# Moving fifteen pairs of gathered rows from the spreading units into the units of pass B's blocks

## The chip, the cores and the metric

The kernel runs on one core of one Trainium2 chip. The metric is the device time of one execution in microseconds. A core has TensorE (PE, the matmuls, with its weight loads as PEld), VectorE (DVE), ScalarE (ACT), GpSimd (POOL), SyncE (SP) and 16 DMA engines that all queues share.

## The reference, cut to what matters

One layer of a trunk over 1024 positions and 1024 features. The second half of it is a product-key expert layer (PEER): each position has 8 heads, and each head picks 16 of 16384 experts.

```python
s1, i1 = lax.top_k(s[:, :, 0], PEER_TOPK); s2, i2 = lax.top_k(s[:, :, 1], PEER_TOPK)
top_s, sel = lax.top_k(cand_s, PEER_TOPK)
idx = jnp.take_along_axis(cand_i, sel, axis=-1)
gate = jax.nn.softmax(top_s, axis=-1)
u = jnp.take(expert_u, idx, axis=0)
act = jax.nn.gelu(jnp.einsum('thkd,td->thk', u, xb))
v = jnp.take(expert_v, idx, axis=0)
return jnp.einsum('thk,thkd->td', gate * act, v)
```

Before it come a gMLP block, a short convolution and an output projection, each with a share of one large input projection.

## The kernel before, in words

The 1024 positions are two groups: A has 3 blocks of 128 positions, B has 5. The expert layer is computed in two ways. For B it is dense: every expert's `u` row is multiplied with every position (64 units of kind E), the chosen gates are **spread** into a dense matrix by one-hot matmuls, and the product is multiplied with every expert's `v` row (64 units of kind W). For A it is sparse: 384 **slots** (3 blocks x 8 heads x 16 experts), and each slot needs one gathered row of `expert_u` and one of `expert_v` for each of 128 positions, 128 rows of 4 KB a gather. So there are 768 gathers, issued by POOL as indirect DMAs (L743), each into a buffer of a ring. DVE uses up each one with one instruction of 128x1024 fp32: a dot product for a `u` row (L1136) or a weighted sum into `acc_sp` for a `v` row (L1145). The buffer is free again after that instruction.

TensorE works through a fixed list of units, `UNITS`. A front unit or an E unit has 96 matmuls of 320 columns (four PSUM tiles; every operand is split into a high and a low fp16 part, which makes three products). In the order of time, for B: V, C, U (4 units), M (16 units, the merged gated products), O (5 blocks, one after another), Q, E, W. The gathers of A are laid beside B's units: `_sections()` gives each unit a number k of slots, and the section of a unit is then about k `u` rows and k `v` rows. The `u` rows run 32 slots ahead of the `v` rows (`LAG`).

The order on each engine is written out by hand, and each engine works strictly in order:

- **DVE, in an M unit**: at odd units the merge (L1290 at u%4 = 1; L1292, L1294, L1297, L1299 at u%4 = 3), which waits for the evacuation of the unit's PSUM tiles; then all rows of the unit's section. After M15's rows come the five blocks of O (`o_block_B`: residual, two layer norms), and then the high and low parts that Q is multiplied with (L1111). The first O block needs x for B, loaded at L660 once M15's tiles are done.
- **ACT, in an M unit**: it evacuates the PSUM tiles into three buffers, which DVE's merges set free.
- **ring of buffers**: 8 buffers for rows in units U and M (`front`), 4 in Q0 and Q1, 6 in the spreading units (`spread`).
- **SP, in U and M**: a 1 MB load of a unit's weights from `hl_dram` (L595), issued four units ahead, when the tiles of the unit that used the buffer before are done.
- **spreading units**: E40 to E59 (`E_SPREAD` = 40, `N_SPREAD` = 20). Beside its 96 matmuls each has 8 spreads of 8 small matmuls (L1922) into `psX`, four PSUM tiles in rotation; ACT copies each spread to `gbuf` (L750, Z<-psX). DVE makes the one-hots, per spread one L1493 and one L1500, and between these it takes rows of the section, one at every second spread. At the end of a unit ACT issues the 2 MB store of `gbuf` (L983, `g_dram`, pieces of 512 bytes) and right behind it the store of the unit's activations (L987, `a_dram`), both on ACT's own DMA queue. Only then does it go on to the copies of the next unit. SP loads 1 MB of `u` weights a unit (L586), which ACT and DVE split (L750, L1040).

Of the kernel before, what the change touches and what calls it, by code (L numbers as in the profile page):

```python
# [191 lines left out]
E_SPREAD = 2 * NGRP - N_SPREAD - 4  # L192
# [12 lines left out]
def _sections():  # L205

    k = {("B", "U", u): 0 for u in (1, 2, 3)}
    for u in range(16):
        k["B", "M", u] = (3 + u % 2) * (u > 0)
    for h in range(HEADS):  # L210
        k["B", "Q", h] = 2 + (h > 1)
    for e in range(2 * NGRP):
        k["B", "E", e] = 2 + e % 2 if e < E_SPREAD - 4 else 2
    groups = NGRP - 2
    left = SLOTS - sum(k.values())
    for g in range(groups):
        k["B", "W", 2 * g] = left * (g + 1) // groups - left * g // groups
    return k

SECTION = _sections()
SEC_UNITS = [u for u in UNITS if u in SECTION]
SEC_OF = {u: c for c, u in enumerate(SEC_UNITS)}
# [1801 lines left out]
```

## Time and profile before

| | us |
|---|---|
| median of 3 runs (lowest, highest) | 2948.1 (2935.65, 2956.32) |
| the profiled execution: its own time | 2951.08 |
| its span, first to last instruction | 2949.3 |
| PE busy | 2828.4 (96%) |
| DVE busy | 2514.4 (85%) |
| ACT busy | 879.7 (30%) |
| POOL busy | 1009.1 (34%) |
| all DMA, mean over the span | 311 GB/s |

### The profile page before, as it was taken

How to read it: one execution, taken by the hardware profiler on the slowest of the kernel's cores; microseconds unless marked ns; L12 is line 12 of the kernel's file. 1: busy time of each engine (PE TensorE's matmuls, PEld its weight loads, DVE VectorE, ACT ScalarE, POOL GpSimd, SP SyncE). 2: the span in 40 equal slices, each digit the busy share in tenths (PEclk: the TensorE clock that was granted, in tenths of full speed). 3: DMA queues.
4: the chain of work that ended last, by engine and by line, in shares of the span. 5: the costliest groups of instructions: out<-in, count | busy, mean ns of one | idle time of the engine just before them, and what ended most of it. 6: DMA issues, size and time to landing. Idle time of an engine off the chain costs nothing.

```text
span 2949.3 us, 47374 instructions
## 1 busy us (share of the span) xinstructions
PE 2828.4 (96%) x19184; PEld 1840.3 (62%) x19184; DVE 2514.4 (85%) x4708; ACT 879.7 (30%) x1321; POOL 1009.1 (34%) x778
## 2 busy tenths in 40 slices
PE   4999999998999899999999989999999999999998
PEld 4566686776677777777776667776544444444443
DVE  6876566987887889999999999997699999999877
ACT  3333542221111342222222334443222222222223
POOL 0000000002776025444445522222465556555410
PEclk9999999999999999999999999999999999999999
DMA  8989653433999468888888899999999999999973
GB/s 328 346 327 379 239 188 129 143 123 131 396 386 379 171 234 313 308 307 316 325 324 321 331 313 327 335 343 309 366 415 414 411 397 411 395 409 403 354 264 136
DMA packets 266236, 917.54 MB, mean 311 GB/s; under 512 B 20465, under 2 KB 102433, under 8 KB 222753
## 3 DMA queue, kind: packets, MB, share of 16 engines
q1 hardware_dynamic: 63968, 427.91, 37.3%
q0 software_dynamic: 110592, 402.70, 36.4%
q10 hardware_dynamic: 91456, 83.89, 8.4%
q8 instruction: 152, 2.49, 0.3%
q14 instruction: 68, 0.55, 0.1%
HBM read 771.79 MB, written 142.63 MB: 310 GB/s over the span
## 4 chain that ended last, share of the span: by engine, by line
PE 37%; DVE 9%; DMA 4%; ACTq 3%; issue 2%; POOL 1%; ACT 1%; DVEq 0%; POOLq 0%
PE psU L1715 6%; PE psU L1716 6%; PE psU L1717 6%; PE psX L1715 5%; PE psX L1717 5%; PE psX L1716 5%; ACTq L987 3%; DMA rows<-in_v_rows,idx_sp 3%; PE psX L1922 2%; DVE acc_sp L1145 2%; DVE w L1040 1%; DMA Z<-in_v_rows,idx_sp 1%; POOL rows L743 1%; DVE rows L1136 1%; DVE Z L1371 1%
## 5 line engine op out<-in xcount | busy, mean ns | idle before, releaser
L1715 PE MATMUL psU<-hB,w 128*128 128x320 f16 (+2 forms) x3104 | 929.8, 300 | 25.3 <-ACT Z L750 11.7
L1716 PE MATMUL psU<-hB,w 128*128 128x320 f16 (+2 forms) x3104 | 929.7, 300 | 0.0
L1717 PE MATMUL psU<-hB,w 128*128 128x320 f16 (+2 forms) x3104 | 929.3, 300 | 0.0
L750 ACT ACTIVATE w<-stage 128x2048 f16<-128x2048 f32 x176 | 335.8, 1909 | 658.9 <-PE psX L1717 347.1
L1040 DVE SCALAR_TENSOR_TENSOR w<-stage,w 128x2048 f16<-128x2048 f32 x176 | 402.6, 2289 | 113.4 <-ACT w L750 113.2
L743 POOL DMA_INDIRECT rows<-in_u_rows,idx_sp x200 | 271.1, 1356 | 382.2 <-DVE rows L1136 234.7
L1715 PEld LDWEIGHTS psU<-hB,w 128*128 128x128 f16 x3104 | 305.8, 99 | 138.9 <-issue 20.8
L1717 PEld LDWEIGHTS psU<-hB,w 128*128 128x128 f16 x3104 | 305.9, 99 | 118.7
L1716 PEld LDWEIGHTS psU<-hB,w 128*128 128x128 f16 x3104 | 305.8, 99 | 111.0
L743 POOL DMA_INDIRECT rows<-in_v_rows,idx_sp x205 | 254.7, 1242 | 277.9 <-DVE rows L1136 178.5
L1715 PE MATMUL psX<-w,Z 128*128 128x512 f16 x768 | 291.1, 379 | 2.5 <-DVE Z L1636 1.4
L1716 PE MATMUL psX<-w,Z 128*128 128x512 f16 x768 | 291.1, 379 | 0.0
L1717 PE MATMUL psX<-w,Z 128*128 128x512 f16 x768 | 291.1, 379 | 0.0
L1145 DVE SCALAR_TENSOR_TENSOR acc_sp<-rows,weight_sp,acc_sp 128x1024 f32<-128x1024 f32 x205 | 258.0, 1288 | 31.9 <-DMA rows<-in_v_rows,idx_sp 26.1
L1715 PE MATMUL psU<-w,Z 128*128 128x512 f16 (+1 forms) x768 | 264.6, 344 | 5.1 <-ACT acc_sp L750 2.6
L1716 PE MATMUL psU<-w,Z 128*128 128x512 f16 (+1 forms) x768 | 264.4, 344 | 0.0
L1717 PE MATMUL psU<-w,Z 128*128 128x512 f16 (+1 forms) x768 | 264.4, 344 | 0.0
L1136 DVE SCALAR_TENSOR_TENSOR rows<-rows,h_sp 128x1024 f32<-128x1024 f32 x200 | 239.2, 1219 | 11.5 <-DMA rows<-in_u_rows,idx_sp 10.3
L750 ACT ACTIVATE R<-psU 128x320 f32<-128x320 f32 (+1 forms) x296 | 123.4, 430 | 310.0 <-PE psU L1717 309.9
L1715 PE MATMUL psU<-Z,w 128*128 128x384 f16 (+1 forms) x640 | 205.7, 321 | 5.7 <-DVE w L1040 5.7
L750 ACT ACTIVATE Z<-psU 128x320 f32<-128x320 f32 (+3 forms) x228 | 96.5, 446 | 367.6 <-PE psU L1717 337.1
L1716 PE MATMUL psU<-Z,w 128*128 128x384 f16 (+1 forms) x640 | 205.6, 321 | 0.0
(262 smaller groups left out, 4432.2 us busy)
## 6 DMA issues: line engine op xcount, KB each, us to landing
stage<-in_u_units SPq DMA_DIRECT2D x64, 1024.0 KB, 8.7
stage<-in_v_units SPq DMA_DIRECT2D x64, 1024.0 KB, 8.0
stage<-in_w_front SPq DMA_DIRECT2D x48, 1024.0 KB, 9.1
hl_dram<-w SPq DMA_DIRECT2D x48, 1024.0 KB, 7.0
w<-hl_dram SPq DMA_DIRECT2D x48, 1024.0 KB, 7.3
a_dram<-R ACTq DMA_DIRECT2D x64, 640.0 KB, 8.0
g_dram<-Z ACTq DMA_DIRECT2D x20, 2048.0 KB, 16.0
Z<-a_dram SPq DMA_DIRECT2D x32, 1280.0 KB, 11.8
```

What stands on the lines that cost most here:

```text
L743: pool.indirect_dma_start(row_at[r], None, u_rows if table == "u" else v_rows, bass.IndirectOffsetOnAxis(ap=idx_sp[:, slot:slot + 1], axis ...
L750: return nc.scalar.activation(dst, src, func, scale=scale)
L987: act.dma_start(a_dram[u // 2, :, 2 * (u % 2):2 * (u % 2) + 2, :], v3(a_ring[:, u % 4, :], 2)).then_inc(a_stored[u % 4], 16)
L1040: V.scalar_tensor_tensor(w[:, n % NW, 1, :], stage[:, v % 2, :], WS, w[:, n % NW, 0, :], ALU.mult, ALU.subtract).then_inc(lo_done, 1)
L1136: V.scalar_tensor_tensor(row_at[r], row_at[r], 1.0, h2_sp[:, slot % SB, :], ALU.mult, ALU.mult, accum_out=dots[:, c % 8, j:j + 1]).then_in ...
L1145: V.scalar_tensor_tensor(dst, row_at[r], weight_sp[:, slot:slot + 1], dst, ALU.mult, ALU.add).then_inc(row_used, 1)
L1371: step(V.max_index(p[:, 8:16], v[:, 8:16], s))
L1715: mm(ps, lhs[0](k), rhs[0](k), start=start and s == 0, stop=False)
L1716: mm(ps, lhs[0](k), rhs[1](k), start=False, stop=False)
L1717: last = mm(ps, lhs[1](k), rhs[0](k), start=False, stop=stop and s == n - 1)
L1922: ins = mm(ps[:, t * P:(t + 1) * P], oh_keys[:, q % 4, t // 2, 0, :, t % 2], oh_gate[:, q % 4, t // 2, c, :, t % 2], start=(c == 0), stop= ...
```

## The change

The number of slots beside an M unit goes from 3 or 4 to 4 or 5 (15 units, M1 to M15), and the number beside E40 to E54 from 2 to 1. E55 to E59 and all other units keep theirs: the W units get what is left of 384 slots, and that is the same number. With the lag, M1 to M15 together get 15 `u` rows and 15 `v` rows more, and E40 to E54 15 of each fewer. Section by section: an odd M unit goes from 4 + 4 rows to 5 + 5, an even one from 3 + 3 to 4 + 4, a spreading unit up to E54 from 2 + 2 to 1 + 1.

```diff
     for u in range(16):
-        k["B", "M", u] = (3 + u % 2) * (u > 0)
+        k["B", "M", u] = (4 + u % 2) * (u > 0)
     for h in range(HEADS):
         k["B", "Q", h] = 2 + (h > 1)
     for e in range(2 * NGRP):
-        k["B", "E", e] = 2 + e % 2 if e < E_SPREAD - 4 else 2
+        k["B", "E", e] = 2 + e % 2 if e < E_SPREAD - 4 else 1 if E_SPREAD <= e < E_SPREAD + 15 else 2
```

## Rows read from the trace of the kernel before

**Rows 1.** The page: GB/s of all DMA in 40 slices of 73.7 us
```profile
GB/s 328 346 327 379 239 188 129 143 123 131 396 386 379 171 234 313 308 307 316 325 324 321 331 313 327 335 343 309 366 415 414 411 397 411 395 409 403 354 264 136
```

**Rows 2.** Windows: us, busy PE, PEld, DVE, ACT, POOL, PEclk, DMA share, GB/s
```profile
770.00:962.00 192.00, 186.16 (x1360) 133.85 (x1357) 153.50 (x193) 25.16 (x69) 128.32 (x107) 0.98 0.99 389
2200.00:2300.00 100.00, 100.00 (x465) 45.36 (x464) 98.14 (x109) 24.79 (x16) 60.31 (x44) 1.00 1.02 415
1680.90:2054.60 373.70, 345.62 (x3203) 265.36 (x3201) 347.06 (x490) 152.62 (x281) 99.95 (x87) 0.96 0.96 321
```

**Rows 3.** DMA view of 770 to 962 us (M1 to M15), slices of 4.8 us
```profile
GB/s 409 416 419 407 411 414 408 414 410 410 410 399 408 412 416 407 411 414 273 274 349 417 376 412 397 356 413 415 417 146 254 393 420 407 415 411 415 396 411 418
DMA packets 18408, 74.77 MB, mean 389 GB/s; under 512 B 2045, under 2 KB 2045, under 8 KB 16539
```

**Rows 4.** SP's timeline, M4 to M15: eleven loads, one at the end of each unit
```profile
824.09 130.69 SPq L595 DMA_DIRECT2D w<-hl_dram  x11
```

**Rows 5.** DVE's groups, 770 to 970 us: busy, mean ns, idle before
```profile
L1136 DVE SCALAR_TENSOR_TENSOR stage<-stage,h_sp 128x1024 f32<-128x1024 f32 x31 | 37.2, 1221 | 10.4 <-DMA stage<-in_u_rows,idx_sp 10.1
L1145 DVE SCALAR_TENSOR_TENSOR acc_sp<-rows,weight_sp,acc_sp 128x1024 f32<-128x1024 f32 x28 | 35.3, 1284 | 7.0 <-DMA rows<-in_v_rows,idx_sp 5.9 <-issue 1.0
...
L1292 DVE SCALAR_TENSOR_TENSOR Z<-Z 128x1280 f32<-128x1280 f32 x4 | 6.0, 1490 | 6.0 <-ACT Z L750 6.0
```

**Rows 6.** DVE's timeline: M15's last rows and the first O block
```profile
967.17 2.48 DVE L1145 SCALAR_TENSOR_TENSOR acc_sp<-rows,weight_sp,acc_sp 128x1024 f32<-128x1024 f32 x2
...
971.44 1.22 DVE L1336 TENSOR_TENSOR R<-R,Z 128x1024 f32<-128x1024 f32 x1 [1.72 <-DMA Z<-in_x]
```

**Rows 7.** Source view of L743: M15's last gather, issued at 951.8 us
```profile
DMA to landing us min/median/max: 11.9/11.9/11.9
```

**Rows 8.** PE's waits, 700 to 1050 us: in total, times, longest
```profile
PE psU L1715 <- ACT Z L750: 9.2, 2, 5.1
PE psU L1715 <- DVE hB L1111: 5.4, 1, 5.4
```

**Rows 9.** PE's waits, 1680 to 2060 us (spreading units)
```profile
PE psX L1922 <- ACT Z L750: 21.4, 11, 4.7
PE psX L1922 <- DVE Z L1500: 6.6, 1, 6.6
```

**Rows 10.** ACT's timeline: the store issued at the end of E40, E41, E42, E56
```profile
1705.93 11.86 ACTq L987 DMA_DIRECT2D a_dram<-R  x1
...
1728.15 6.00 ACTq L987 DMA_DIRECT2D a_dram<-R  x1
...
1744.86 12.27 ACTq L987 DMA_DIRECT2D a_dram<-R  x1
...
1996.02 12.65 ACTq L987 DMA_DIRECT2D a_dram<-R  x1
```

**Rows 11.** Source view of L987, 1700 to 2060 us: ns min/median/max of an issue
```profile
L987 ACTq DMA_DIRECT2D a_dram<-R x20: 5537/8445/12648, 1705.9 to 2055.1; - x20
```

**Rows 12.** PE's timeline: its wait in E43, behind the third of those issues
```profile
1758.02 0.59 PE L1922 MATMUL psX<-Z 128*128 128x128 f16 x4 [4.34 <-ACT Z L750]
```

**Rows 13.** Windows, PE alone: us, busy, PEclk, DMA share, GB/s, at that wait
```profile
1755.80:1762.60 6.80, 4.58 (x26) 0.50 0.94 365
```

**Rows 14.** DMA view of 1706 to 1718 us, by queue: packets, MB, share
```profile
q10 hardware_dynamic: 3761, 1.92, 53.8%
q0 software_dynamic: 567, 2.08, 47.4%
```

**Rows 15.** DMA view of 1728 to 1734 us, the same (q10: ACT's, q0: POOL's)
```profile
q10 hardware_dynamic: 2805, 1.44, 85.5%
q0 software_dynamic: 87, 0.29, 11.9%
```

**Rows 16.** DVE's groups, 1700 to 2060 us
```profile
L1493 DVE TENSOR_TENSOR Z<-Z 128x1024 f16<-128x1024 f16 x152 | 103.9, 684 | 13.6 <-PE psX L1922 13.6
L1040 DVE SCALAR_TENSOR_TENSOR w<-stage,w 128x2048 f16<-128x2048 f32 x20 | 45.8, 2288 | 10.0 <-ACT w L750 9.9
```

## The prediction

> **What bounds the kernel now.** I read the windows first, then the DMA view of the same stretches, then the waits, and the timelines at the places where the change acts. By the page [rows 1] the DMA engines carry 379 to 396 GB/s in slices 11 to 13, where the M units are, and 307 to 344 in slices 24 to 28, where the spreading units are; the stretch of W moves 415 [rows 2]. In both stages that the change touches PE is nearly full (186 of 192 us; 346 of 374) and so are the DMA engines (share 0.99 and 0.96) [rows 2]. So two things are to be asked: what 30 more gathers cost where they go, and what 30 fewer give where they come from.
>
> M stage: PE needs 13.04 us a unit: ten units lie between the first and the last of eleven loads that are issued as units end, (130.69 - 0.3) / 10 [rows 4]. DVE has idle time, but spends it waiting for gathers: 10.1 us before the u rows in the `stage` buffers, 5.9 before the v rows in `rows` [rows 5]. In 32 of 40 slices the DMA view reads 396 to 420 GB/s, 411 on average; the low slices (146, 254, 273, 274) are the few moments when the ring was full [rows 3]. I take 412 GB/s as what the engines can do with this mixture. The stage is thus just short of a DMA bound. What comes after it is not covered: DVE goes from M15's last row (ends 969.6) to the first O block with a wait of 1.7 us, and that wait is for a load and not for PE [rows 6]; at the end of the five O blocks PE is the one that waits for DVE, 5.4 us (L1111) [rows 8]. So DVE's rows in M15 lie on the path that sets the end, one to one but for 1.7 us.
>
> Spreading stage: a unit without a wait takes 1744.86 - 1728.15 = 16.71 us [rows 10]. Twenty of them are 334.2; the stage takes 373.7 [rows 2], 39.5 more. E40 starts the one-hots and takes 1705.9 - 1680.9 = 25.0, of which 8.3 are its own start (6.6 of it a wait for L1500 [rows 9]); 31.2 are left for E41 to E59. They begin as waits for ACT's copies, 21.4 us in 11 waits [rows 9]. ACT is not busy then: it sits in the issue of the `a_dram` store, behind the 2 MB `g_dram` store on the same queue, for 5.5 to 12.6 us, half of the times over 8.4 [rows 11]. PE can go on with four `psX` tiles before it misses the copies: an issue of 12.27 became a wait of 4.34 [rows 10, 12], the longest issue of 12.65 goes with the longest wait of 4.7 [rows 9, 10], so PE waits for the issue's length less 7.9 us. A long wait is followed by a stretch at the lower of TensorE's two clocks (1.2 GHz), granted clock 0.50 for 6.8 us [rows 13]; these stretches are the other 10 of the 31 us.
>
> **Part 1, 15 u and 15 v rows more in M1 to M15.** Three prices, and the largest counts. DVE: a row takes 1.22 or 1.28 us, 1.24 in a chain [rows 5, 6], and a unit's merges five instructions of up to 1.49 in four units [rows 5]. Four units are 36 x 1.24 + 7.0 = 51.6 us, against 4 x 13.04 = 52.2 of PE: just covered, no cost. POOL: 107 gathers cost 128.3 us [rows 2], 1.20 each, with 0.3 us between two; 9 a unit are 13.5 us, 0.5 a unit over PE. DMA: 30 gathers of 128 x 4 KB are 15.73 MB. Added to the 74.77 MB of the stretch they are 90.5 MB, and at 412 GB/s 219.7 us, where it now takes 192 [rows 3]. That is 27.7 us, the largest, and holds the other two. Today M15's last gather lands at 951.8 + 11.9 = 963.7 [rows 7] and its row starts at 968.4 (the second of the pair that starts at 967.17 [rows 6]), so 4.7 us of lead are used up first, then the 1.7 us of the wait for x. The cost on the path is 27.7 - 4.7 - 1.7 = **21.3 us**. From both sides: at 420 GB/s, the best slice, 215.5 us and a cost of 17; at 400, as with some bubbles left, 226.3 and 28. PE's own wait behind a merge and its clock dip in M4 (about 7 us) are inside that and are not paid again. Weight loads have a lead of three units (39 us) and stay hidden.
>
> The Trainium skill bears on this in "DMA: Bandwidth & Descriptors", section "Where 436 GB/s comes from": it puts the fabric's ceiling at 435 GB/s and says that for HBM to SBUF the HBM side binds at about 358. The trace does not agree with the second figure: the stage already moves 389 on average and 415 at W. By the skill's 435 the sum would be 208 us, an estimate, and the cost on the path some 10; by its 358 it would be 253 us and a cost of 54.
>
> **Part 2, 15 u and 15 v rows fewer in E40 to E54.** DVE's work a unit is now 8 x 2 x 0.68 for the one-hots, 2.29 for L1040 and 4 x 1.25 for rows [rows 5, 16], 18.2 and about 17 with the overlap of short instructions: over PE's 16.71. Two rows fewer make it 14.6: DVE is no bound any more, and its one-hots run ahead of PE. The DMA engines move only 321 GB/s at a share of 0.96 [rows 2], since the 512 byte pieces of the `g_dram` store take more engine time a byte. Of the 12 us issue, the gathers took 2.08 MB and 47% and the store 1.92 MB and 54% [rows 14]; in the 6 us issue the store had 85% and the gathers 12% [rows 15]. So the length of the issue is the time in which the store gets rid of some 1.4 to 1.9 MB, and the gathers that run beside it set the rest. With half as many gathers the median of 8.4 should fall to 6 to 7.5 us, below the 7.9 from which PE waits. What is lost in E41 to E54: 31.2 less the 8.5 that belong to E55 to E59 (the wait of 4.7 behind the issue of 12.65 at 1996.0 [rows 10], a clock dip of at most 3.4 after it, and small ones), so 22.7 us. E41 keeps some of its wait, since POOL fills the ring of six at the start of the stage as before: 3.5 us with the clock. For E55 to E59, which keep two slots but start from an emptier queue, I count 2 of the 8.5. The gain is 22.7 - 3.5 + 2 = **21 us**, from 6 (only DVE's surplus over PE, 14 x 0.4) to 31 (all of it).
>
> **Part 3, everything else.** The sections from E55 on hold the same number of rows with other slot numbers; Q0 to E39 too. POOL's first gathers of Q and E sections have leads of many us and move with the rest. Nothing is removed from W, which takes over where PE ends.
>
> **The sum** on the profiled execution of 2951.1 us: + 21.3 - 21.0 = 2951. That execution is 3 us above the median of the runs, 2948.1, so I expect **2949 us**.
>
> **Rivals.**
> 1. *The spread does not shrink.* Slower, and one mechanism: the issue on ACT's queue is set by the store's own descriptors and by the `u` load (L586) beside it, which stay; then issues stay above 7.9 us and PE waits on. For it: the store and the load are there in every unit, and short issues follow units in which PE had just waited. Against it: rows 14 and 15. Its price: gain 6, cost 21 to 28: 2963 to 2971. It decides when the median issue in E41 to E54 stays above 8 us.
> 2. *M is not bound by DMA.* DVE's waits and the low slices take in the gathers, and M costs what POOL lacks: 15 x 0.5 = 7.5 us, or 1 after the leads of 6.4. For it: the low slices [rows 3]. Against it: they are few. With a cost of 5 it is 2949 - 16 = 2933, with all of the 31 us as gain too 2923.
> 3. *389 GB/s is the limit.* The slices above it are bursts, the reads from HBM can't hold more than the mean of the stretch [rows 2]: 90.5 MB are 232.6 us, 40.6 more, 34.2 on the path, and 2951.1 + 34.2 - 21.0 less the 3 are 2961. For it: the mean stayed at 389 with DVE waiting. Against it: 18 slices in a row hold 399 to 419 [rows 3], and W holds 415 for 100 us. The skill's 358 of the section named above is this mechanism with a lower number.
> 4. *The change doesn't do what it says*: the rows in a spreading unit are taken at the first odd spreads, so the remaining two could both fall into ACT's issue. Then it is rival 1 with a gain of 10 or so.
>
> **How the numbers follow.** Forecast 0.60; rivals 1 and 4 together 0.20; rival 2 0.15; rival 3 0.05. Nearly all of it lies within 1% (29.5 us), about what a measurement of this kernel tells from no change: below 2919 only if M costs nothing and the whole 31 are gained (0.04); above 2977 with a rate under 400 and hardly any gain, or with rivals 1 and 3 together (0.08). The range takes the bounds of both parts, 17 to 28 and 6 to 31, and some us for the spread of the runs, without their corners: 2930 to 2970.
>
> **What would show it.** Right: 770 to about 990 us at 405 to 415 GB/s without low slices; DVE waits for gathers in most M units, PE for ACT at each fourth; M15's last row ends near 991; E41 to E54 at 16.7 us a unit, L987 at 6 to 7.5 us. Wrong: low slices left in M and its end near 975 (rival 2), or L987 above 8 us in the units with one slot (rival 1).

## The result, and the profile after

| | before | changed |
|---|---|---|
| median, us (lowest, highest; 20 runs each) | 2947.8 (2935.7, 2966.9) | 2967.9 (2952.9, 2975.1) |
| ratio, 95% interval | | 1.0063 [1.0046, 1.0079] |
| profiled execution: span | 2949.3 | 2972.5 |

The changed kernel is 0.6% slower, about 19 us; a later series (e10 below) gave 1.0044 [1.0009, 1.0079]. The forecast of 2949 was 19 us too low. The measured time lies inside the range (2930 to 2970), 2 us under its upper end, and inside "within 1%".

To see where the 23 us between the two spans arose, I divided both executions at the end of the same pieces of work. The places are read in the timelines of DVE and PE: M0's and M15's last row, E39's last row, then the end of PE's unit E40, E54 and E59. The other kernels of this study are in the same table, since most of what follows is read from it. "Again" marks a second profile of a kernel.

| us | M0's rows end | M0 to M15 | M15 to E39 | to E40 | E40 to E54 | E54 to E59 | to the end | span |
|---|---|---|---|---|---|---|---|---|
| before | 778.4 | 191.2 | 715.5 | 20.6 | 256.5 | 92.4 | 894.7 | 2949.3 |
| changed | 778.3 | 228.9 | 719.4 | 21.7 | 233.9 | 93.0 | 897.3 | 2972.5 |
| changed, again (e10) | 779.6 | 230.3 | 707.5 | 22.0 | 234.4 | 89.6 | 896.0 | 2959.4 |
| x late (e5) | 780.3 | 225.9 | 700.7 | 20.6 | 233.9 | 85.6 | 898.6 | 2945.6 |
| half bytes, again (e11) | 780.8 | 211.1 | 720.1 | 21.6 | 233.9 | 91.2 | 895.8 | 2954.5 |
| half DVE, again (e12) | 777.8 | 220.9 | 717.5 | 20.7 | 233.9 | 89.9 | 895.0 | 2955.6 |
| both halves (e9) | 778.8 | 188.8 | 702.5 | 20.9 | 234.3 | 87.0 | 895.4 | 2907.7 |
| seven to W (e6) | 779.1 | 190.4 | 714.2 | 21.1 | 247.2 | 85.8 | 897.2 | 2934.9 |
| four to M (e7) | 783.4 | 194.1 | 726.8 | 22.1 | 249.0 | 91.3 | 899.0 | 2965.7 |
| spread, half bytes (e8) | 779.7 | 190.3 | 704.2 | 20.8 | 239.3 | 85.9 | 902.0 | 2922.3 |
| M only (e1) | 776.3 | 255.3 | 714.5 | 21.7 | 257.5 | 87.2 | 898.7 | 3011.1 |
| spread only (e2) | 778.4 | 213.6 | 714.6 | 20.7 | 234.8 | 87.2 | 914.4 | 2963.7 |
| half bytes (e3) | 782.3 | 230.1 | 717.1 | 21.3 | 233.9 | 86.8 | 899.2 | 2970.6 |
| half DVE (e4) | 778.7 | 289.3 | 720.6 | 21.3 | 235.9 | 86.3 | 895.3 | 3027.4 |

The M units cost 37.7 us and E40 to E54 gave 22.6 back; everything else together is 8.1 (3.9 + 1.1 + 0.6 + 2.6, less 0.1). One column teaches a caution: from M15 to E39 no two kernels differ in what they do (e5 alone moves a load at its very start), and yet the stretch takes 701 to 727 us. A difference of 10 us between two single spans is therefore nothing. M and E40 to E54 repeat better: 191.2, 190.4 and 190.3 us in M where its slots are those of before (before, e6, e8; e2 has waits in M that are told below), and 233.9 to 234.8 us from E40 to E54 in eight of the nine kernels that have one slot there with whole gathers (235.9 in e4). So a difference of a few us can be read there.

The windows of the changed kernel, for [rows 2] (us, busy PE, PEld, DVE, ACT, POOL, PEclk, DMA share, GB/s):

```profile
770.00:1006.00 236.00, 201.22 (x1446) 144.46 (x1445) 198.19 (x249) 26.44 (x74) 162.61 (x140) 0.93 1.01 396
1715.70:2075.20 359.50, 340.34 (x3203) 263.76 (x3201) 318.13 (x447) 153.46 (x281) 65.27 (x58) 0.97 0.91 296
2200.00:2300.00 100.00, 100.00 (x465) 45.32 (x464) 97.69 (x108) 22.59 (x15) 61.03 (x43) 1.00 1.01 409
```

The DMA view of 770 to 1006, for [rows 3] (slices of 5.9 us, then the sum):

```profile
GB/s 415 417 407 410 412 408 417 408 409 409 419 403 417 405 412 411 410 405 297 332 374 405 421 408 412 412 407 412 279 330 399 405 409 411 409 415 408 411 388 307
DMA packets 23504, 93.49 MB, mean 396 GB/s; under 512 B 2560, under 2 KB 2560, under 8 KB 21647
```

The slices are near 410, as forecast, but the low ones are not gone (297, 332, 374, 279, 330, 307), and the stretch holds 93.5 MB where I had counted 90.5. The three low places come behind the merges of M7, M11 and M15 (L1292 to L1299, from 867.1, 927.2 and 990.0 on): for their 5.3 us DVE uses no row, no buffer comes free, and POOL stands. (M3's merge, from 806.9 on, has none behind it; there SP had just issued three loads of 0.5 MB.) This is POOL's timeline at the first of them:

```profile
873.93 1.68 POOL L743 DMA_INDIRECT stage<-in_v_rows,idx_sp  x1 [4.52 <-DVE stage L1136]
875.92 1.98 POOL L743 DMA_INDIRECT stage<-in_v_rows,idx_sp  x1 [0.30 <-issue]
```

From there to 889.2 it issues eleven gathers, 1.53 us apart, without another wait, while the slices read 297 to 374. DVE's waits from 770 to 990, for [rows 5] (total, times, longest):

```profile
DVE acc_sp L1145 <- DMA rows<-in_v_rows,idx_sp: 12.3, 10, 2.8
DVE acc_sp L1145 <- DMA stage<-in_v_rows,idx_sp: 10.0, 9, 2.2
DVE rows L1136 <- DMA rows<-in_u_rows,idx_sp: 6.4, 5, 2.5
```

PE's waits from 700 to 1070, for [rows 8]:

```profile
PE psU L1715 <- ACT Z L750: 26.4, 4, 9.7
PE psU L1715 <- DVE Z L1299: 11.5, 1, 11.5
PE psU L1715 <- DVE hB L1111: 5.4, 1, 5.4
```

PE now stands 9.7 us where it stood 5.1, because DVE comes late to the merge at every fourth unit and ACT then has no free buffer. That is a symptom: in the changed kernel PE ends M15 at 974.3 and DVE its rows 33 us later. At their end x was long there, for [rows 6] (DVE's timeline):

```profile
1002.21 5.00 DVE L1145 SCALAR_TENSOR_TENSOR acc_sp<-stage,weight_sp,acc_sp 128x1024 f32<-128x1024 f32 x4
1007.14 0.15 DVE L1158 SCALAR_TENSOR_TENSOR weight_sp<-dots,gate_sp 128x4 f32<-128x4 f32 x1
1007.21 1.21 DVE L1336 TENSOR_TENSOR R<-R,Z 128x1024 f32<-128x1024 f32 x1
```

In the spreading units the issue of the `a_dram` store shrank. ACT's timeline at the end of E40 and E41, the source view of L987 over all 20 units (ns min/median/max), and PE's waits of that stage, for [rows 10], [rows 11] and [rows 9]:

```profile
1748.48 6.51 ACTq L987 DMA_DIRECT2D a_dram<-R  x1
1765.18 5.95 ACTq L987 DMA_DIRECT2D a_dram<-R  x1
```
```profile
L987 ACTq DMA_DIRECT2D a_dram<-R x20: 5274/5954/11828, 1748.5 to 2075.7; - x20
```
```profile
PE psX L1922 <- DVE Z L1500: 13.2, 1, 13.2
PE psX L1922 <- ACT Z L750: 6.0, 2, 3.9
```

All fourteen units from E41 to E54 take 16.71 us. The one long wait left (13.2 us, in E40) is no cost of its own: E40 ends 20.6 to 22.1 us after DVE's last row of E39 in every kernel of the table, wherever PE stood.

### The profile page after: what moved, and what is told of

It is laid out like the page before. It is cut to its first block, busy times and chain, and to the rows that moved or that the text cites. A ratio compares the mean times of both kernels' runs of the same rounds, so it can differ in the third digit from the quotient of the medians.

```text
span 2972.5 us, 47374 instructions
## 1 busy us (share of the span) xinstructions
PE 2832.7 (95%) x19184; PEld 1841.9 (62%) x19184; DVE 2520.3 (85%) x4708; ACT 880.7 (30%) x1321; POOL 1006.3 (34%) x778
## 4 chain that ended last, share of the span: by engine, by line
PE 39%; DVE 16%; DMA 7%; issue 3%; POOL 3%; ACT 1%; ACTq 1%; DVEq 0%; POOLq 0%
PE psU L1715 7%; PE psU L1716 7%; PE psU L1717 7%; PE psX L1716 5%; PE psX L1715 5%; PE psX L1717 5%; DMA rows<-in_v_rows,idx_sp 3%; DVE acc_sp L1145 3%; DMA Z<-in_v_rows,idx_sp 3%; PE psX L1922 2%; DVE w L1040 2%; POOL rows L743 1%; DVE rows L1136 1%; DVE Z L1371 1%; DVE Z L1361 1%
## 5 line engine op out<-in xcount | busy, mean ns | idle before, releaser
L743 POOL DMA_INDIRECT rows<-in_u_rows,idx_sp x196 | 260.0, 1326 | 402.6 <-DVE rows L1136 318.2
L743 POOL DMA_INDIRECT rows<-in_v_rows,idx_sp x203 | 259.4, 1278 | 271.6 <-DVE rows L1136 149.1
L1136 DVE SCALAR_TENSOR_TENSOR rows<-rows,h_sp 128x1024 f32<-128x1024 f32 x196 | 234.6, 1221 | 17.2 <-DMA rows<-in_u_rows,idx_sp 16.2
```

Source lines behind the costliest of these rows:

```text
L743: pool.indirect_dma_start(row_at[r], None, u_rows if table == "u" else v_rows, bass.IndirectOffsetOnAxis(ap=idx_sp[:, slot:slot + 1], axis ...
L1136: V.scalar_tensor_tensor(row_at[r], row_at[r], 1.0, h2_sp[:, slot % SB, :], ALU.mult, ALU.mult, accum_out=dots[:, c % 8, j:j + 1]).then_in ...
```

## The experiments

**First series: the two halves of the change, and two ways to relieve M.** Four kernels on one chip, where the kernel before had a median of 2961.6.

e1, the M part alone (15 slots come out of W):

```diff
-        k["B", "M", u] = (3 + u % 2) * (u > 0)
+        k["B", "M", u] = (4 + u % 2) * (u > 0)
```

> Only the first half of the change: M1 to M15 get one slot more, the spreading units keep two, and the W units get 15 slots fewer. Theory (the two halves are separate costs, M pays 37 us in DMA time): DVE's last row of M15 ends near 1007 us as in the changed kernel, E40 to E59 keep their waits (about 370 us in all), and the time is that of before plus 32 to 38 us, about 2982, W giving back at most 5. Rival (the long M stage is partly made up for later, in the units that DVE leads): plus 20 or less.

e2, the spreading part alone (15 slots go to W):

```diff
-        k["B", "E", e] = 2 + e % 2 if e < E_SPREAD - 4 else 2
+        k["B", "E", e] = 2 + e % 2 if e < E_SPREAD - 4 else 1 if E_SPREAD <= e < E_SPREAD + 15 else 2
```

> Only the second half: E40 to E54 have one slot, M as before, the W units get 15 slots more. Theory: E41 to E54 take 16.71 us each and the store issues (L987) 6 us, so the stage ends 22 us earlier; W, where DVE is at 98%, takes 15 to 25 us longer for its 15 slots, so the sum is within 8 us of before. Rival (the spreading units are short only because M shifted everything): issues stay at 8 us and over and E41 to E54 keep 10 us or more of waits.

Measured: e1 3009.1 us, ratio 1.0141 [1.0079, 1.0202]; e2 2966.1, ratio 1.0003 [0.9972, 1.0034]. e2 came out as its theory expected; e1 cost 47 us, more than the 32 to 38 expected, and its last row of M15 ended at 1031.6 and not near 1007. In the spreading units both read cleanly: 257.5 us in e1, 234.8 in e2, as before and as in the changed kernel. Fifteen slots in W made its stretch 914.4 instead of 894.7, 19.7 us. But M took 213.6 us in e2, whose M section is that of before, against 191.2. PE's waits of e1 from 765 to 1000 show something that neither first profile has:

```profile
PE psU L1716 <- issue: 10.7, 18, 1.1
PE psU L1715 <- issue: 8.2, 19, 1.0
PE psU L1717 <- issue: 7.5, 13, 1.0
```

PE stood 50 times for 0.5 us each with nothing to wait for that the profile shows; in e2 it was 12.6 us in 22 waits. So the price of the M part can only be read here as e1 less e2, 41.7 us, and not against before; and as e1 has 14 us more of these waits than e2, that is rather too much.

e3, the changed kernel with gathers of half a row in M1 to M15 (the other half is what lay in the buffer):

```diff
+                half = SEC_UNITS[ROWS[m][2]][1] == "M" and SEC_UNITS[ROWS[m][2]][2] > 0
+                src = u_rows if table == "u" else v_rows
-                pool.indirect_dma_start(row_at[r], None, u_rows if table == "u" else v_rows,
+                pool.indirect_dma_start(row_at[r][:, 0:HT] if half else row_at[r], None,
+                                        src.rearrange("e (a n) -> (e a) n", a=2) if half else src,
```

> The changed kernel with gathers of 2 KB instead of 4 KB a row for the rows of M1 to M15: the same number of instructions on POOL and DVE, half of the bytes (the gathered data is other data, and half of each buffer is stale). Theory (M is bound by DMA bytes): M1 to M15 go at PE's 13.04 us a unit, DVE's last row of M15 ends at 970 to 980 us, and the time is 27 to 36 us under the changed kernel, about 2937. Rival (POOL's 1.5 us a gather or DVE's rows are the bound): the row ends at 990 or later, and less than half of the 37 us goes.

e4, the changed kernel with whole gathers, of which DVE uses half the columns in M1 to M15:

```diff
+                n_ = HT if SEC_UNITS[c][1] == "M" and SEC_UNITS[c][2] else D
-                V.scalar_tensor_tensor(row_at[r], row_at[r], 1.0, h2_sp[:, slot % SB, :], ALU.mult, ALU.mult,
+                V.scalar_tensor_tensor(row_at[r][:, 0:n_], row_at[r][:, 0:n_], 1.0, h2_sp[:, slot % SB, 0:n_], ALU.mult, ALU.mult,
```

> The changed kernel with DVE using only 512 of 1024 columns of each row in M1 to M15: same gathers and bytes, DVE's row time halved (the other half of the dot products and sums is left out). Theory (DMA bytes): DVE waits for gathers instead, the last row of M15 ends at 998 to 1007 us, the time is at most 9 us under the changed kernel. Rival (DVE at 1.24 us a row is the bound): it ends near 975 and the time falls by 25 us or more.

Measured: e3 2965.2, ratio 1.0016 [0.9975, 1.0057], M 230.1 us; e4 3030.7, ratio 1.0224 [1.0169, 1.0279], M 289.3 us. e3 misses what the theory expected (its last row of M15 ended at 1012.3, as the rival had it), but 22 us of waits named issue stand in its M, so it decides nothing; e4 misses both expectations. With half of DVE's work M took 289.3 us against the 228.9 of the changed kernel, which no account of DVE, DMA and POOL gives. PE's waits of e4, 765 to 1060:

```profile
PE psU L1720 <- issue: 23.2, 29, 2.4
PE psU L1718 <- issue: 22.0, 27, 2.4
PE psU L1719 <- issue: 19.7, 23, 1.7
```

65 us of the same kind, and the mean granted clock from 780 to 1000 is 0.82 (0.92 in the changed kernel). My theory at this point was that gathers which never pause starve TensorE's instruction supply. The last series tests it.

**Second series: the x load, smaller doses, and bytes in the spreading units.** Another chip, before 2948.7. None of the four has waits named issue.

e5, the changed kernel with the load of x for B in five pieces, four of them after M's last row:

```diff
-            sp.dma_start(x2["B"], x[NTOK["A"]:S].rearrange("(b p) d -> p b d", p=P)).then_inc(x2_in["B"], 16)
+            sp.dma_start(x2["B"][:, 0, :], x[NTOK["A"]:NTOK["A"] + P]).then_inc(x2_in["B"], 16)
+            sp.wait_ge(row_used, FRONT_ROWS)
+            for b in range(1, DB):
+                sp.dma_start(x2["B"][:, b, :], x[NTOK["A"] + b * P:NTOK["A"] + (b + 1) * P]).then_inc(x2_late[b], 16)
```

(Not shown: DVE waits for `x2_late[b]` before block b.)

> The changed kernel, with x for B loaded in five pieces: the first block as before once M15's tiles are done, the other four (2.1 MB) only after the last row of M15. Theory (every MB that runs beside the last gathers of M delays the O blocks by 1 MB / 0.41): DVE's last row of M15 ends 4 to 6 us earlier than with one load, and the time is 3 to 6 us under the changed kernel, ratio to before about 1.005. Rival (the O blocks then wait for their pieces): no gain, DVE waits for in_x between blocks.

Measured: 2965.1, ratio 1.0083 [1.005, 1.0115]; M 225.9 us, 3.0 and 4.4 under the two profiles of the changed kernel, where 4 to 6 were expected. The stretch shows the 3 us, the time does not: its interval cannot separate 3 us. (The span of 2945.6 is a short M15 to E39, 700.7.)

e6, before with one slot fewer in E40, E42 to E52 (every second), seven slots to W:

```diff
-        k["B", "E", e] = 2 + e % 2 if e < E_SPREAD - 4 else 2
+        k["B", "E", e] = 2 + e % 2 if e < E_SPREAD - 4 else 1 if e in range(E_SPREAD, E_SPREAD + 14, 2) else 2
```

> Before, with one slot fewer in seven spreading units (E40, E42, ... E52) and these seven in the W units, M untouched. Theory (every second unit with half the gathers keeps the issue of the store under 7.9 us; W takes some 7 slots at no cost, since 15 cost 20 us and DVE is at 98%): the stage ends 12 to 18 us earlier, W takes 0 to 8 us longer, the time is 6 to 15 us under before (ratio 0.995 to 0.998). Rival (the waits come back in each unit that keeps two): under 8 us of gain in the stage, ratio 1.000 or over.

e7, before with one slot from each of E40, E42, E44, E46 to M6, M8, M10, M12:

```diff
-        k["B", "M", u] = (3 + u % 2) * (u > 0)
+        k["B", "M", u] = (3 + u % 2) * (u > 0) + (u in (6, 8, 10, 12))
-        k["B", "E", e] = 2 + e % 2 if e < E_SPREAD - 4 else 2
+        k["B", "E", e] = 2 + e % 2 if e < E_SPREAD - 4 else 1 if e in range(E_SPREAD, E_SPREAD + 8, 2) else 2
```

> Before, with one slot fewer in E40, E42, E44 and E46 and one more in M6, M8, M10 and M12. Theory (M's DMA had 10 us of low slices, which 4.2 MB nearly fill): M15's rows end 2 to 7 us later, the spreading stage is 8 to 14 us shorter, the time 3 to 10 us under before (ratio 0.997 to 0.999). Rival (the cost is proportional, 2.5 us a slot): M15's rows end 10 us later, ratio 1.000 or over.

Measured: e6 2945.9, ratio 1.0007 [0.997, 1.0044]; e7 2952.1, ratio 1.0033 [0.9996, 1.007]. In e6 E40 to E54 took 247.2, 9.3 less (12 to 18 were expected), and the median issue was still 8.4 us; its end stretch is 2.5 longer. In e7 M cost only 2.9 us more for four slots, and E40 to E54 gave 7.5 (8 to 14 were expected). So by the stretches that they touch e6 should be 6.8 us faster than before and e7 4.6, and neither median shows it. The interval of e6 (down to 0.997, 9 us) leaves room for its gain, that of e7 hardly. What eats it is open: single profiles can't show what the stretch M15 to E39 does on average.

e8, before with gathers of half a row in E40 to E54 and nothing moved:

```diff
+                half = kind_ == "E" and E_SPREAD <= u_ < E_SPREAD + 15
```

(The gather itself is then edited as in e3.)

> Before, with gathers of 2 KB instead of 4 KB a row in E40 to E54: as many gathers and DVE rows as before, the bytes of the change (half of each buffer is stale and the values are of other rows). Theory (the waits are the store's issue on ACT's queue, and its length is DMA traffic): issues fall to 6 to 7.5 us, PE's waits for ACT are gone from E42 on, and the units take 17.0 to 17.2 us, DVE's own time, instead of 18.0 on average; 12 to 16 of the 22.6 us come back. Rival (DVE's row time makes the waits): issues stay at 8 to 12 us and under 6 us come back.

Measured: 2933.0, ratio 0.9958 [0.9923, 0.9994]. The windows of before, of the changed kernel and of e8 from E40's end to E54's, and then e8's source view of the `a_dram` store, which is L991 there:

```profile
1705.70:1962.20 256.50, 240.71 (x2243) 185.13 (x2241) 243.08 (x344) 106.56 (x198) 65.86 (x58) 0.97 0.99 328
```
```profile
1748.30:1982.20 233.90, 233.90 (x2242) 182.62 (x2241) 211.04 (x296) 107.31 (x197) 32.06 (x28) 1.00 0.92 293
```
```profile
1695.10:1934.40 239.30, 237.31 (x2242) 180.39 (x2241) 237.35 (x338) 107.38 (x198) 64.63 (x57) 1.00 0.90 292
```
```profile
L991 ACTq DMA_DIRECT2D a_dram<-R x15: 5406/5609/8501, 1695.3 to 1934.6; - x15
```

With all rows still there and half of their bytes gone, 17.2 of the 22.6 us come back and the issue falls to 5.6 us. That is more than the 12 to 16 that the theory expected. DVE is busy 237 of 239 us, so the 5.4 us that remain fit DVE's own pace; no wait in PE's view names it. In this stage the bytes are the cause of the long issue, and that is shown.

**Third series: M, all four combinations on one chip.** A third chip, before 2954.8. e9 has the edits of e3 and e4 together; e10, e11 and e12 are the changed kernel, e3 and e4 again.

> The changed kernel with both halvings in M1 to M15: the gathers bring 2 KB of a 4 KB row, and DVE uses 512 of 1024 columns (so the output of those rows is not the reference's). Theory: the matmuls that stood without a cause in the half-DVE kernel (59 us of waits named issue in the profile's rows) did so because the gathers never paused once DVE no longer held them back; with half the bytes the DMA engines have room, so these waits are under 15 us in all, PE is the bound with its 13.0 us a unit, and M15's last row ends at 970 to 985. Rival: DVE's pace or the order of the rows causes them, and bytes have no part; then they stay above 40 us and M15's last row ends above 1020.

> The changed kernel itself, once more, so that the two kernels with half rows stand beside it in one series. Theory: no waits named issue beside M, M15's last row ends at 1003 to 1010 as in the first profile, the DMA engines move 395 to 400 GB/s, and the ratio to the kernel before is 1.004 to 1.009. Rival: the four kernels of the first series had such waits because of the chip on which they ran, and not because of what was edited; if this chip is such a one too, the waits show up here as well, 10 to 30 us of them, and M15's last row ends above 1015.

> The changed kernel with gathers of 2 KB instead of 4 KB in M1 to M15, once more (half of each row is what lay in the buffer). Theory, that the DMA engines set the pace of M: if there are no waits named issue here, DVE's waits for gathers fall from 34 us to under 12, PE's three waits of 26 us behind the merges go, and M15's last row ends at 985 to 995, which is DVE's own 15 sections of work behind PE's units; the ratio to the kernel before is 0.997 to 1.002. Rival, that DVE's work sets the pace and its gather waits only take up slack: M15's last row stays above 1000.

> The changed kernel with DVE's row instructions on 512 of 1024 columns in M1 to M15, once more (so the output of those rows is not the reference's); the gathers are whole. Theory: as in the first series, gathers that never pause go with waits of TensorE that are named issue, 40 us or more of them, and M15's last row ends above 1040. Rival: those waits belonged to the chip of the first series; here they are under 10 us, and the stage is bound by the bytes: 15 sections' 90 MB at 412 GB/s, M15's last row near 985.

Measured: e9 2909.5 (one run), e10 2965.3, ratio 1.0044 [1.0009, 1.0079], e11 2955.6, ratio 1.0019 [0.9981, 1.0057], e12 2957.4 (one run). No kernel of this series has a wait named issue in M. PE's waits of e12, 765 to 1000, beside those of e4, the same kernel:

```profile
PE psU L1718 <- ACT Z L750: 18.2, 3, 11.0
PE psU L1718 <- DVE Z L1302: 10.5, 1, 10.5
PE psU L1718 <- DMA w<-hl_dram: 2.2, 1, 2.2
```

The theory of starvation falls: e12 gathers without a pause and has none of these waits; the rival, that they belonged to the first series and not to the edit, holds. e9's last row of M15 ended at 967.6, 2 us before the theory's 970 to 985, but that says nothing for starvation any more. e11 ended in its range, at 991.9, with more waits for gathers than expected (21 us, not under 12), and PE's waits behind the merges did not go but fell from 32 us (e10) to 17; e12 at 998.8, later than the rival's 985. The windows of 770 to 990 of e10, e11, e12 and e9, in this order:

```profile
770.00:990.00 220.00, 193.33 (x1385) 137.31 (x1383) 179.97 (x228) 24.49 (x69) 154.17 (x132) 0.95 1.01 399
```
```profile
770.00:990.00 220.00, 202.20 (x1454) 144.88 (x1453) 195.46 (x250) 26.53 (x75) 171.39 (x142) 0.95 0.80 266
```
```profile
770.00:990.00 220.00, 189.08 (x1369) 135.08 (x1367) 124.87 (x239) 24.06 (x68) 134.57 (x135) 0.94 1.02 410
```
```profile
770.00:990.00 220.00, 216.78 (x1650) 161.61 (x1649) 146.57 (x282) 31.73 (x88) 150.85 (x141) 0.99 0.82 284
```

| M0 to M15, us (less the 191.2 of before) | whole rows gathered | half rows gathered |
|---|---|---|
| DVE uses whole rows | 228.9 and 230.3 (+38 to +39) | 211.1 (+20) |
| DVE uses half rows | 220.9 (+30) | 188.8 (-2) |

This table is the answer on M. The two cells with half of DVE's work rest on one run each. With DVE's rows halved the DMA engines are the bound, at 410 GB/s without one slice under 395, and the added bytes cost 30 us.

With half of the bytes the DMA engines have room (266 GB/s), and the added rows still cost 20 us. What sets the pace there is read from who waits. DVE is busy 195 of 220 us and waits 21 us for gathers, all before 946; POOL, which issues the gathers, hardly waits at all. DVE's waits of e11 from 778 to 1000 and POOL's one long wait from 770 to 990, behind M15's merge:

```profile
DVE acc_sp L1148 <- DMA stage<-in_v_rows,idx_sp: 12.6, 7, 4.2
DVE acc_sp L1148 <- DMA rows<-in_v_rows,idx_sp: 8.0, 3, 3.9
```
```profile
POOL stage L745 <- DVE stage L1139: 5.7, 3, 4.5
```

POOL's 136 gathers of M1 to M15 take 213.2 us in e11: 166.4 in the gathers, 0.3 between every two, and 5.7 of waiting beyond that. In e9 they take 190.1: 147.0 in the gathers and 2.0 of waiting. The issue is longer where DVE does more beside it, as the source view of the gathers (L745) shows for e11 (772 to 986) and e9 (770 to 960.4), ns min/median/max:

```profile
L745 POOL DMA_INDIRECT rows<-in_v_rows,idx_sp x36: 942/1382/1990, 783.7 to 972.8; - x36
L745 POOL DMA_INDIRECT stage<-in_v_rows,idx_sp x32: 942/1360/1990, 779.3 to 983.4; - x32
```
```profile
L745 POOL DMA_INDIRECT rows<-in_v_rows,idx_sp x36: 942/947/1924, 781.4 to 950.6; - x36
L745 POOL DMA_INDIRECT stage<-in_v_rows,idx_sp x32: 942/964/2214, 777.4 to 959.5; - x32
```

In e11 the 47 gathers whose issue lies mostly beside a dot product of a whole `u` row (L1139) take 1.57 us on average, the 65 beside a sum of a `v` row 0.98, and the 5 with no instruction of DVE beside them 0.95. So DVE's rows act on M in two ways, by their own time and by what they add to POOL's; e11 and e9 change both at once, and no run separates them. In the lower right cell POOL's 190.1 us still fit into what PE needs (15 x 13.04 = 195.6 us). Together the two edits' prices are 38, more than the dearer one and less than their sum.

## Why the prediction was right, and where its steps were off

**The sign of each part and the balance**: right in kind, since a cost in M and a gain in the spreading units came at the places named, and nothing else moved by more than the scatter. The balance of +0.3 us was +15 in the two stretches (37.7 - 22.6), because the cost was mis-sized. That the range held is in part luck: a cost of 37.7 lies outside its own bounds (17 to 28), the 22.6 of gain took the edge off, and the measured 2968 is also what rival 1 had forecast (2963 to 2971) by a mechanism that did not happen. (The sum as written, 2951.1 + 21.3 - 21.0 less 3, is 2948.4; I gave 2949.)

**Part 1, the term that was off.** I had 21.3 us on the path and M15's last row near 991; it ended at 1007.2 (and 1009.9 in the second profile), a cost of 37.7. Of the 16.2 us, by the DMA view, some 7 are bytes: 93.5 MB instead of 90.5, and 3.0 MB at 412 GB/s are 7.3 us. SP's queue, with the x load, moved 2.0 MB more than in rows 3 (19.27 against 17.26), and POOL's 16.7 more (74.00 against 57.30), 1.0 above the 15.73 of the 30 gathers. So the x load of 2.6 MB makes up most of the 3.0; 0.6 of it were inside the 74.77 that I had started from. It hangs on PE's end of M15 (issued at 974.3), so once DVE's rows trail PE by more it no longer follows the last gathers but runs beside them. I had named that load as what DVE waits for, and had not asked when it starts in the changed kernel. The other 9 are the rate: 93.5 MB at 396 are 236 us, at 412 227. e12 agrees with both from the other side: with half of DVE's work the rate is 410 and the last row ends at 998.8, which is 991 and the extra bytes. e5 took away the x load and got 3.0 to 4.4 of the 7 back.

**The step that failed in Part 1** is "three prices, and the largest counts". DVE was costed at nothing, because four units are 51.6 us of its work against 52.2 of PE, and POOL at 13.5 us a unit, 0.5 over PE, which the DMA time was to hold. With the bytes halved the rest costs 20 us (e11), and it is POOL that does not wait there: 1.22 + 0.3 us a gather and 5.7 us of waiting are 213.2 us for 136 gathers, against 15 x 13.04 = 195.6 of PE. I had priced POOL's gathers as if they did not depend on DVE; by e11 and e9 they do (1.22 and 1.08 us on average). Beside the DMA bound the same thing costs the last 8 to 9 us (e12): at the merge of each fourth unit the ring of 8 stays full for 4.5 us, and behind it POOL's gathers come 1.53 us apart (in e12, behind M7's merge, 1.26). There lie the low slices, which I had expected to vanish; in e12 POOL stands for 4.0 us at these merges too, and no slice is low. That a faster POOL alone would shorten M is read from these waits; no run tried it.

**Part 2: right, by its mechanism.** E41 to E54 at 16.71 us a unit, issues of 5.7 to 7.7 us there (forecast 6 to 7.5), and no wait for ACT's copies. The gain was 22.6, from the 22.7 that I had counted as lost there; my deduction of 3.5 for E41 was not needed, and the 2 for E55 to E59 can't be read: that stretch is 92.4 before, 93.0 and 89.6 in the two profiles of the changed kernel, and 87.2 in e1, whose spreading units are those of before. The rule "issue less 7.9" held where an issue was long: 11.83 gave a wait of 3.9. e8 shows that the gathers' bytes set the issue, and it puts DVE's surplus, for which I had 14 x 0.4 = 5.6, at 5.4.

**Part 3**: the stretches that I called unchanged differ by 0.6 to 3.9 us each, which is less than they scatter; nothing can be read from it.

**The rivals.** 1 is out: the median issue is under 8 us. 2 is out as a whole, as M ended at 1007 and not near 975, though its doubt on the low slices was where my rate failed, and its engine, POOL, is the one that sets the pace in e11. 3 is out: e12 carried 410 GB/s through the stretch. The Trainium skill ("DMA: Bandwidth & Descriptors", section "Where 436 GB/s comes from") has about 358 for HBM to SBUF; the trace of e12 disagrees, with 410 over 220 us, and stays under that section's fabric ceiling of 435. 4 is out: in the first profile no unit with one slot had an issue above 7.7 us, and in the other kernels with one slot in all of E40 to E54 those above 8 us are at most three of fifteen (one of 8.3 in e10). In e6, where every second unit keeps two, one-slot units had up to 9.1.

**What stays open.** The waits named issue of the first series; how the 20 us of e11 divide between DVE's own time and POOL's; and why e6 and e7, shorter in their own stretches, have the median of before. Moving slots did not beat the kernel before in any version; e2, with the slots in W, is level with it, since W lost 19.7 us where E40 to E54 gained 21.7, and would be the better half of the change.

## What to carry to other kernels

Where two engines are each within a few per cent of being the bound, price the work moved to that stage as more than the largest of their prices: here 20 and 30 alone were 38 together. Before calling an engine covered, look at who waits for whom with the bound taken away, since the price of one engine's instruction can depend on what another does beside it. When a stage gets longer on one engine, look for loads that another engine's progress releases, as they will land in the middle of it. And to learn whether bytes or instructions are what a stage pays for, halve each by itself and then both, on the same chip, and compare the stretch and not the span.

## What the runs showed of the hardware beyond that

- The same kernel (e4 and e12) took 289.3 and 220.9 us in M on two chips. In the slower execution PE stood 79 times for 65 us in all with nothing to wait for in the rows, 2.4 us at the longest, and the granted clock fell to 0.82; in the other not once. All four kernels of that series had such waits (13 to 65 us in M), none of the ten other profiles did. In e1, e2 and e4 all of them lie where the DMA engines are busy 92% or more of the time, but in e3, with half of the bytes (238 GB/s in M), 24 of its 35 lie below 90%. Whether the chip or that hour is the cause is not known; a comparison across series would have put it down to the edit.
- A gather's issue on POOL took 0.94 us in each of the 28 cases of the kernel before in which no instruction of DVE ran beside it, and up to 1.99 us beside DVE's row instructions of 1024 columns.
- The DMA engines held 410 GB/s for 220 us with gathers of 4 KB rows beside 1 MB loads.
- The second of two stores on ACT's queue took 8.4 us to issue at the median beside 4 KB gathers at two slots a unit, 5.6 with the same gathers at 2 KB, and 5.95 with half as many gathers; ACT can do nothing in that time.
